# Recurrence: old x added by an identity product in TensorE's accumulation, x copied by VectorE, gates by tanh, w2 loaded in long runs

## What is computed

```python
dec = w0 + tanh(xw @ w1) @ w2                       # for both directions z
w = exp(-exp(-softplus(-dec) - 0.5))                # decay
a = sigmoid(a0 + (xa @ a1) @ a2)
kt = k * (1 + (a - 1) * k_a)
S_f, y_f = _rwkv_scan(S0[0], (r, w[0], kk, kk * a[0], kt[0], v), False)   # first to last token
S_b, y_b = _rwkv_scan(S0[1], (r, w[1], kk, kk * a[1], kt[1], v), True)    # last to first
bonus = sum(r * kt * r_k) * v

gate, idx = lax.top_k(aff, cap)                      # each expert takes its 64 best tokens
hid = silu(xin @ w1) * (xin @ w3)
y = (hid @ w2) * gate                                # added to the tokens' rows
```

## Time and profile before

| | |
|---|---|
| median of 3 runs | 3452.81 us (3449.86 to 3456.63) |
| the profiled execution | 3458.04 us |
| its span, first to last instruction | 3456.2 us |
| busy: TensorE, its weight loads, VectorE | 3112.5, 1799.8, 1644.0 us |
| busy: ScalarE, GpSimd | 836.5, 283.2 us |
| the scan, first to last product | about 2297 to 2815 us |
| the last mixture, loads at some 410 GB/s | about 2960 to 3440 us |

### The profile page before, as it was taken

The page is one execution under the profiler, slowest core; times in us unless marked ns, Lnnn a source line. Parts: engine busy times, 40 slices in busy tenths (PEclk is TensorE's granted clock), DMA queues, the critical chain, the costliest instruction groups (busy, mean ns, idle before and its releaser), DMA issues. The chain is left out here.

```text
span 3456.2 us, 72498 instructions
## 1 busy us (share of the span) xinstructions
PE 3112.5 (90%) x31846; PEld 1799.8 (52%) x31846; DVE 1644.0 (48%) x3491; ACT 836.5 (24%) x1909; POOL 283.2 (8%) x297
## 2 busy tenths in 40 slices
PE   6998999989799999599999979998989878798887
PEld 5855658546344565343333335557888864232322
DVE  4574635656454586411112154238888866222211
ACT  2103410134211372100000010137766641000000
POOL 0000000000011110000000000001222230000000
PEclk9998999999899999699999989989999998899999
DMA  6564135720311223599999922100000034799998
GB/s 186 151 204 154 26 86 154 207 92 26 112 50 56 69 72 120 200 374 390 392 388 393 347 82 73 43 1 5 5 5 5 5 118 171 276 406 401 409 405 350
DMA packets 148762, 605.32 MB, mean 175 GB/s; under 512 B 17408, under 2 KB 20032, under 8 KB 131936
## 3 DMA queue, kind: packets, MB, share of 16 engines
q1 hardware_dynamic: 143424, 583.38, 45.9%
q0 software_dynamic: 5024, 17.30, 2.1%
HBM read 578.50 MB, written 28.44 MB: 176 GB/s over the span
## 5 line engine op out<-in xcount | busy, mean ns | idle before, releaser
L2126 PE MATMUL psum<-ring,big 128*32 128x256 f32 (+1 forms) x2688 | 386.5, 494 | 24.9 <-DMA ring<-moe_w 11.6
L2126 PE MATMUL psum<-front,big 128*32 128x256 f32 (+1 forms) x2384 | 320.3, 480 | 10.9 <-DMA front<-moe_w 6.4
L441 PE MATMUL psum<-h_uT,ring 128*128 128x264 f32 x1280 | 290.5, 387 | 0.0
L570 DVE SCALAR_TENSOR_TENSOR h_O<-h_O,cond_silu 128x512 f32<-128x512 f32 x336 | 227.0, 745 | 102.3 <-DMA h_O<-ada_w 102.3
L2126 PEld LDWEIGHTS psum<-ring,big 128*32 128x32 f32 (+1 forms) x2688 | 134.5, 124 | 267.2 <-issue 218.2
L441 PEld LDWEIGHTS psum<-h_uT,ring 128*128 128x128 f32 x1280 | 242.0, 190 | 46.5 <-issue 5.8
L2265 DVE TENSOR_TENSOR big<-big,psum 128x512 f32<-128x512 f32 (+1 forms) x48 | 28.7, 599 | 443.8 <-PE psum L2126 431.3
L2126 PEld LDWEIGHTS psum<-front,big 128*32 128x32 f32 (+1 forms) x2384 | 114.1, 122 | 208.8 <-issue 174.5
L2204 ACT ACTIVATE big<-psum 128x512 f32<-128x512 f32 (+1 forms) x48 | 23.5, 524 | 643.4 <-PE psum L2126 643.4
L2754 PE MATMUL psum<-ring,gates 64*64 64x128 f32 (+1 forms) x5120 | 169.4, 253 | 5.9 <-issue 4.1
L461 PE MATMUL psum<-ring,h_uT 128*128 128x512 f32 x384 | 168.3, 595 | 0.0
(11 more groups left out here) (453 smaller groups left out, 5152.4 us busy)
## 6 DMA issues: line engine op xcount, KB each, us to landing
ring<-moe_w SPq DMA_DIRECT2D x84, 2048.0 KB, 12.8
front<-moe_w SPq DMA_DIRECT2D x67, 2048.0 KB, 12.9
big<-moe_w SPq DMA_DIRECT2D x28, 2048.0 KB, 28.2
h_O<-ada_w SPq DMA_DIRECT2D x192, 256.0 KB, 2.9
ring<-w_in SPq DMA_DIRECT2D x16, 2048.0 KB, 13.1
X<-moe_w SPq DMA_DIRECT2D x13, 2048.0 KB, 12.1
ring<-na_w_qkv SPq DMA_DIRECT2D x6, 2048.0 KB, 7.9
ring<-w_out SPq DMA_DIRECT2D x4, 2048.0 KB, 9.1
```

The costliest lines, as they stand in the source:

```text
L441: last = nc.tensor.matmul(bank(k, pair_bank(q) + h, NH), w[:, a, f * P:(f + 1) * P], uT[:, a, halves[h]], start=a == 0, stop=a == KD - 1)
L570: nc.vector.scalar_tensor_tensor(into, ada(u), by, into, ALU.mult, ALU.add).then_inc(s.acc, 1)
L2126: last = nc.tensor.matmul(bank(k, b, r.width)[q * r.n:(q + 1) * r.n, :], rowsT[:, half * HALF_K + n, r.first:r.first + r.n], w[:, n, q * r ...
```

## The change

Five things change.

1. `up` is now `raise_x`: after the four products of a pair index come four more of 64x64, with a 64x64 identity (`k.eye2`) as one operand and the old x as the other, into the same place in PSUM, so that PSUM holds x + M x. VectorE copies instead of adding: two copies of 128x256 in levels 1 to 4, one of 128x512 in levels 5 and 6. The exchanged halves change back in the identity product, so x stays in one place, and `n_and_x` and `x_of_side` go.
2. The gates are 0.5 tanh(v / 2) + 0.5: ScalarE computes the tanh, GpSimd the rest in place (`gate`). `cumulate` and VectorE's `key_scale` wait for GpSimd now. GpSimd's order in a slot: `decayed`, `end`, dec gate, `akk`, iclr gate, the bonus product.
3. The bonus sum is made in two halves of 64 columns, 8 products.
4. w2 of the last mixture is loaded with rows 4p to 4p + 3 of a half on partition p, 16 KB side by side.
5. To match, `flip_hid` there turns every fourth column of `hid`.

```diff
@@ expert_chunk
+    if j >= 4 and l == DEPTH - 1:
+        half = D // 2
+        return d[name][l, e, (j - 4) * half:(j - 3) * half, :].rearrange("(p a) n -> p a n", p=P)
@@ experts, flip_hid
-                for m in range(r.width // P):
-                    at = wide(r).start + m * P
-                    last = nc.tensor.transpose(bank(k, r.ups, P, m * P), hid[:, at:at + P], k.ident[:, :])
+                blocks = r.width // P
+                mine = hid[:, wide(r)]
+                by_row = mine.rearrange("q (p m) -> q m p", m=blocks) if NS == 1 else mine.rearrange("q (m p) -> q m p", m=blocks)
+                for m in range(blocks):
+                    last = nc.tensor.transpose(bank(k, r.ups, P, m * P), by_row[:, m, :], k.ident[:, :])
@@ rwkv_scan, GpSimd
+            def gate(z, t, who, name, tile):
+
+                made("act", z, t, who)
+                fr["pool"][z].done(nc.gpsimd.tensor_scalar(own(tile, z), own(tile, z), 0.5, 0.5, ALU.mult, ALU.add), t, name)
...
+                if m is not None:
+                    gate(y, m, "decay_tanh", "dec_gate", T_dec)
                 if f is not None:
                     rates(z, f)
-                    if lat(f):
-                        bonus_in(z, f)
+                if m is not None:
+                    gate(y, m, "iclr_tanh", "iclr_gate", T_rate)
+                if f is not None and lat(f):
+                    bonus_in(z, f)
@@ rwkv_scan, TensorE
+            def raise_x(z, m, with_n):
+
+                width = 2 * CH if with_n else CH
+                right = n_with_x(z) if with_n else x_of(z)
+                for i in range(QUAD):
+                    for b, p, flip in ((U(z), i, False), (U(z) + 1, QUAD + i, True)):
+                        pair(b, 0, p, [(m, right)], flip, stop=False, width=width)
+                    for b, p, flip in ((U(z), i, False), (U(z) + 1, QUAD + i, True)):
+                        at = p % QUAD * width + width - CH
+                        for h in range(2):
+                            lo = h * CH
+                            to = (1 - h if flip else h) * CH
+                            last = nc.tensor.matmul(bank(k, b, CH, at)[to:to + CH, :], one(lo, p), x_of(z)(lo, p), start=False, stop=True)
+                return last
...
+            one = lambda lo, p: k.eye2[lo:lo + CH, :]
...
-                made("act", z, t, "decay_gate")
+                made("pool", z, t, "dec_gate")
...
-                    last = nc.tensor.matmul(bank(k, W(z) + 1, 2, SIDE + 2 * i), own(T_dec, z)[:, i * P:(i + 1) * P], k.head_ones[:, 0:P:CH], start=True, stop=True)
+                    for g in range(2):
+                        at = i * P + g * CH
+                        last = nc.tensor.matmul(bank(k, W(z) + 1, 2, SIDE + 2 * i)[g * CH:(g + 1) * CH, :], own(T_dec, z)[:, at:at + CH],
+                                                k.head_ones[:, 0:P:CH], start=True, stop=True)
...
-                if n < LEVELS - 1:
-                    last = heads(U(z), 0, (m, with_x(z, n % 2 == 0)), width=2 * CH)
-                else:
-                    last = heads(U(z), 0, (m, x_alone(z, n % 2 == 0)))
-                ev["pe"][z].done(last, t, f"up{n}")
+                ev["pe"][z].done(raise_x(z, m, n < LEVELS - 1), t, f"up{n}")
@@ rwkv_scan, ScalarE
-                fr["act"][z].done(nc.scalar.activation(own(T_dec, z), own(T_dec, z), ACT.Sigmoid), t, "decay_gate")
+                fr["act"][z].done(nc.scalar.activation(own(T_dec, z), own(T_dec, z), ACT.Tanh, scale=0.5), t, "decay_tanh")
@@ rwkv_scan, VectorE
             def step(z, t, n):
                 after("pe", z, t, f"up{n}")
-                got = woven(U(z), 1) if n < LEVELS - 1 else side(U(z), 0)
-                x = X(z)[:, 0, :, :]
-                ev["dve"][z].done(tt(x, x, got[:, 0, :, :], ALU.add), t, f"xlow{n}")
-                if n < LEVELS - 1:
-                    after("act", z, t, f"Nhigh{n}")
...
-                    last = tt(new[there], old[here], got[there, 1, :, :], ALU.add)
-                ev["dve"][z].done(last, t, f"x{n}")
+                x = X(z)
+                if n >= LEVELS - 1:
+                    ev["dve"][z].done(nc.vector.tensor_copy(x, side(U(z), 0)), t, f"x{n}")
+                    return
+                got = woven(U(z), 1)
+                ev["dve"][z].done(nc.vector.tensor_copy(x[:, 0, :, :], got[:, 0, :, :]), t, f"xlow{n}")
+                after("act", z, t, f"Nhigh{n}")
+                ev["dve"][z].done(nc.vector.tensor_copy(x[:, 1, :, :], got[:, 1, :, :]), t, f"x{n}")
```

More of the change, by code:

```diff
@@ L2608, in scan_events @@
         act=["rows", "x0"] + [f"{x}{n}" for n in range(1, LEVELS - 1) for x in ("M", "Nhigh", "N")] + [f"M{LEVELS - 1}"],
-        dve=["mask_m"] + only("mask_ar") + ["mask_b"] + only("mask_br") + ["x0", "mask_n"] + [f"{x}{n}" for n in range(1, LEVELS + 1) for x in ("xlow", "x")]
+        dve=["mask_m"] + only("mask_ar") + ["mask_b"] + only("mask_br") + ["x0", "mask_n"] + [f"{x}{n}" for n in range(1, LEVELS + 1) for x in (("xlow", "x") if n < LEVELS - 1 else ("x",))]
             + only("y", "y_carried") + ["state"],
@@ L2613, in scan_events @@
         pe=["dec", "iclr", "cumulate"] + only("bonus"),
-        act=["decay_gate", "iclr_gate", "d_exc", "d_inc", "d_inv"],
+        act=["decay_tanh", "iclr_tanh", "d_exc", "d_inc", "d_inv"],
         dve=["dec", "iclr", "alpha", "m", "kt", "kappa", "beta"] + only("rho", "bonus"),
-        pool=["akk"] + only("bon", "bonus_in") + ["end"])
+        pool=["dec_gate", "iclr_gate", "akk"] + only("bon", "bonus_in") + ["end"])
     return chain, front
@@ L2639, in rwkv_scan @@
     N, X = (lambda z: joint4(NX, z, 0)), (lambda z: joint4(NX, z, 1))
-    def n_and_x(z, p, other):
-        n = z * D + 2 * p * CH
-        apart = 2 * D + z * BANK + p * CH - n if other and p >= QUAD else CH
-        return near[:, n:n + 2 * apart].rearrange("p (e x) -> p e x", e=2)[:, :, 0:CH]
-    def x_of_side(z, other):
-        return pairs(T_dx, z)[:, QUAD:, :] if other else joint(NX, z, 1)[:, QUAD:, :]
     U, W = (lambda z: 4 * z), (lambda z: 4 * z + 2)
@@ L2939, in _, with decay_tanh, iclr_tanh @@
             copy = lambda out, got: nc.scalar.activation(out, got, ACT.Copy)
-            def decay_gate(z, t):
+            def decay_tanh(z, t):
                 made("dve", z, t, "dec")
-                fr["act"][z].done(nc.scalar.activation(own(T_dec, z), own(T_dec, z), ACT.Sigmoid), t, "decay_gate")
-            def iclr_gate(z, t):
+                fr["act"][z].done(nc.scalar.activation(own(T_dec, z), own(T_dec, z), ACT.Tanh, scale=0.5), t, "decay_tanh")
+            def iclr_tanh(z, t):
                 made("dve", z, t, "iclr")
-                fr["act"][z].done(nc.scalar.activation(own(T_rate, z), own(T_rate, z), ACT.Sigmoid), t, "iclr_gate")
+                fr["act"][z].done(nc.scalar.activation(own(T_rate, z), own(T_rate, z), ACT.Tanh, scale=0.5), t, "iclr_tanh")
             sums = lambda z, e: bank(k, U(z), 2 * BANK).rearrange("p (a e x) -> p a e x", e=2, x=CH)[:, :, e, :]
@@ L2987, in slot @@
                 if m is not None:
-                    decay_gate(y, m)
+                    decay_tanh(y, m)
                 if i is not None:
@@ L2991, in slot @@
                 if m is not None:
-                    iclr_gate(y, m)
+                    iclr_tanh(y, m)
                 if i is not None:
@@ L3028, in key_scale @@
             def key_scale(z, t):
-                made("act", z, t, "iclr_gate")
+                made("pool", z, t, "iclr_gate")
                 if t:
@@ L3089, in step @@
                 after("pe", z, t, f"up{n}")
-                got = woven(U(z), 1) if n < LEVELS - 1 else side(U(z), 0)
-                x = X(z)[:, 0, :, :]
-                ev["dve"][z].done(tt(x, x, got[:, 0, :, :], ALU.add), t, f"xlow{n}")
-                if n < LEVELS - 1:
-                    after("act", z, t, f"Nhigh{n}")
-                if n == 1:
-                    after("dve", z, t, "x0")
-                else:
-                    after("dve", z, t, f"x{n - 1}")
-                old, new = x_of_side(z, n % 2 == 0), x_of_side(z, n % 2 == 1)
-                for h in range(2):
-                    here, there = slice(h * CH, (h + 1) * CH), slice((1 - h) * CH, (2 - h) * CH)
-                    last = tt(new[there], old[here], got[there, 1, :, :], ALU.add)
-                ev["dve"][z].done(last, t, f"x{n}")
+                x = X(z)
[6 more added lines that the diff above has]
+                ev["dve"][z].done(nc.vector.tensor_copy(x[:, 1, :, :], got[:, 1, :, :]), t, f"x{n}")
             def slot(z, i, f, y, j, n, m):
```

3 lines of the change are left out of this document (1 added, 2 removed).

## The result

| | before | changed |
|---|---|---|
| median | 3454.72 us (3449.86 to 3458.32, 4 runs) | 3582.14 us (3565.11 to 3592.17, 4 runs) |
| ratio, 95% interval | | 1.0363 [1.0334, 1.0392] |
| the profiled execution | 3458.04 us | 3590.72 us |
| its span | 3456.2 us | 3588.9 us |

The change makes the kernel 127 us slower. I forecast 3556 with a range of 3475 to 3590, so the sign and the range held and the size was 26 us short.

The account below looks back on a forecast made before the run. The prediction took the supply of TensorE's instructions to bound the scan, at about 3.6 us a packet. Its terms, +106 + 2 - 6 + 1 = +103 us on 3452.8, gave 3556 us, range 3475 to 3590.

Parts of the forecast that it names:

- A: The forecast: in the scan TensorE's instruction supply sets the pace, 3.4 to 3.75 us a packet, 3522 to 3589; chance 0.80.
- (1): In the scan, identity products and bonus sum bring 35.4 more instruction packets at 3.6 us each: +106 us.
- (2): In the scan, TensorE's time in the identity products: 75 us against 39.1 us of waits; not added to (1).
- (3): Bonus sum in the scan, as half-wide products: -8 us of arithmetic or 0; only its 256 instructions count, in (1).
- (4) to (6): In the scan: VectorE 70 us less, ScalarE 59 us less, GpSimd two more operations a slot; zero in the sum.
- (7): Last stage, w2 loaded in 16 KB instead of 4 KB pieces: -6 us, between 0 and -8.
- (8): Last stage, hidden rows turned from a strided view: 4 us of TensorE, taken as +1, between 0 and 4.
- B: Rival: TensorE's arithmetic alone counts, with a second instruction packet already under way: 3475 to 3494; chance 0.13.
- C: Faster rival: the scan's TensorE-ScalarE-TensorE level chain leads; 144 x - 60, x us for a level's products, below 0.37; chance 0.03.
- D: No-change rival: the same level chain in the scan as C, with x between 0.37 and 0.46, 3453; chance 0.03.

Follow-up runs that it names:

- tiny16: Kernel before plus 16 products of 64x2 weights and 2 columns ahead of each level's second product, all on one array quarter: 3615.50 us, ratio 1.0433.
- best: Kernel before with tanh gates, long w2 rows, strided turning, and 16 low-rank iclr products joined to 8 of 128 weight columns: 3465.96 us, ratio 1.0015.
- no_id: Changed kernel without the identity products, so the old x is left out and it computes something else: 3446.95 us, ratio 0.9959.
- gates_w2: Kernel before with only the tanh gates, the long w2 rows and the strided turning: 3442.62 us, ratio 0.9978.
- id_wide: Changed kernel with each level's 16 identity products of 64 columns joined into 4 of 256, behind the sixteen others: 3486.91 us, ratio 1.0085.

## Why the prediction was right, and where it fell short

**What bounds the kernel.** Right. With equal columns and fewer instructions the scan's loss fell from 125 us to 33; with equal instructions and less arithmetic it was 117. In eleven of the thirteen kernels the packets come every 3.65 to 3.79 us; tiny16 and best, where TensorE's own work per packet was raised most, take longer. The forecast said 160.4 packets and there were 160. The range of 3475 to 3590 held the result, 3582, by 8 us; A's own span ended at 3589.

**(1), the mis-sized term.** I took 3.6 us a packet, "the middle of the two stops", and had 577 us. Measured were 596.2, 3.73 a packet: 19 of the 26 us. The mean of before, 3.77, was the better number. I had read it as arithmetic with some slack and looked for the bound below it, between two single intervals of 3.2 and 4.0 us. But intervals of a comb vary: single ones go down to 3.25 us in the changed kernel too, under a mean of 3.73. No kernel's mean over the middle went under 3.65. Before lay at 3.77 and so near the bound, as no_id shows; much of its 39 us of waits for ScalarE was time in which the next packet was on its way anyway. gates_w2 still has 34 us of those waits at a pace of 3.71, so the bound itself isn't one fixed number.

**The remaining 7 us.** The scan's edges count 55.2 us in both kernels only because the middle was cut that way. Cut by work instead, from VectorE's first operation on x in slot 1 to that in slot 24, the 23 slots took 472.6 us before and 599.3 now, 127 more, and from there to the scan's end 24.0 and 23.5: the 24th slot cost nothing more, where I had put +2. The rest gave -6.0 for -5. Beside the 19 of the first cut, which has the edges at 0, that makes -3. Another 2 us are before's own median (3454.7 now, 3452.8 then). The other 8 lie ahead of the scan or in the scatter of runs; nothing in the code answers to them.

**(2), (3).** The arithmetic is real: 0.43 to 0.54 us a level. That it is hidden entirely is by the model, in which it runs while the next packet comes. The trace splits the middle's 125 us into 79 of busy time (500.7 for 421.3) less some 31 of waits for data, and 76 of stops. So the supply has at least the 76, and id_wide's 92 by another way; of the rest no run tells arithmetic from supply. The bonus sum's half-wide products run at 16 in 0.56 us (2767.80 to 2768.36 in the changed kernel's timeline) for 1.0 before. That is the 0.5 expected. No run has it alone; no_id, which has it and the gates, is 1.3 us shorter in the scan.

**(4) to (6).** -69 us for -70 on VectorE; -48 for -59 on ScalarE; both without gain, as said. GpSimd's gate cost half of what I put, and no wait of TensorE names it among the first.

**(7), (8).** -6 was expected and -6.0 measured. The w2 load comes in pieces of 16 KB, and the whole stretch went from 407 to 412 GB/s. That w2's own stretches now run at 426, as forecast, wasn't read off: all pieces have one size now, and the packets don't tell w2 from w1. The turned rows now come from a strided view and cost 213 ns a load:

```profile
L2149 PEld LDWEIGHTS psum<-ident_sb,big x64: 195/213/221, 3114.2 to 3563.8; 128*128 128x128 f32 x64
```

That is 73 ns more than the earlier trace rows, 64 x 0.073 = 4.7 us, just above the upper end of (8). The stretch as a whole still gained.

**The rivals.** B (3475 to 3494) is refuted: the change took 3582, with 107 stops of up to 1.7 us, 80.7 us in all, the long ones at the borders of packets. C and D come from 144 x - 60. With x = 0.48, as measured in the change, they give +9 and it lost 127; id_wide, with x = 0.43, would have been 2 us slower by that and was 30 slower, so the chain was not what led.

By the Trainium skill, "Runtime: NRT & Kernel Launch", section "Instruction fetch mechanics", the crossing from one 16 KiB block to the next is mostly hidden. The changed kernel's trace disagrees, with the 80.7 us of stops just named; in the kernel before they came to 7.2 us.

**A slot** was to take 26 to 27 us for some 22. Over the 23 slots it is 599.3 / 23 = 26.1, for 20.5 before.

**What stays open.** Why the same scan runs at 3.71 us a packet in one kernel and 3.78 in another (up to 9 us in the scan) isn't settled, nor what keeps a second packet from being under way ahead of time. How the 33 us of id_wide divide between supply and arithmetic isn't either. Whether another placement of the program in memory changes the pace wasn't tried. A trade that would make the identity products pay, fewer and wider main products, wasn't found: they all have weights of their own.

## What to carry to other kernels

Before adding small products to a stage where TensorE looks 90% busy, count its instructions (products and weight loads) against the packets of kind "instruction". If the stage already takes about 3.7 us for each 16 KB packet, as here, every further 256 instructions cost about that much even where their arithmetic would take less, and more where it takes longer (tiny16, 3.97; best, 3.93). Time saved on other engines was worth next to nothing here. Idle time put down to "issue" in the middle of a run of equal products is the sign of it, and the mean interval of a long stretch is the price, not the shortest one. If such products are needed, join those that share their weights: the same columns in 4 products for 16 cost 33 us of the scan here instead of 125.

## What was not expected of the hardware

- The supply of TensorE's program: one packet of 16.4 KB every 3.65 to 3.79 us over the middle of the scan in eleven kernels, with no data on the DMA engines (share 0.02). Where TensorE stops for one, the next starts only about 1 us after it has gone on, and the long stops lie multiples of 256 instructions apart.
- Products of 2 columns are not cheap on one quarter of the array: 27 ns a record (0.87 us for 32), against 9 ns spread over four quarters (0.29 us) and some 16 ns for 64 columns spread (0.52 us).
- Weights of 64x128 against 64x64: 120 ns a record (1.93 us for 16) against about 29 (0.93 us for 32), with the same 64 columns moving.
- A fused multiply and add by constants on GpSimd, 128x512: 617 ns, half the 1.27 us of a product of two tensors of that size.
- w2 in pieces of 4 KB for 16 KB, 21862 DMA packets for 12051 in 400 us: some 1% of the rate, 407 for 412 GB/s, in one execution of each.
